# Experts' tokens beyond 128: small blocks of 32 on raw weights in four column groups instead of blocks of 64 on split weights

## The chip, the cores and the metric

One core of a Trainium2 chip runs the whole kernel. The metric is the device time of one execution in microseconds, from its first to its last instruction and what lies around them. Five engines work side by side: TensorE (PE, with its weight loads PEld), VectorE (DVE), ScalarE (ACT), GpSimd (POOL) and SyncE (SP, which here only issues loads). They meet at semaphores. Sixteen DMA engines move data.

## What is computed

One layer of a hybrid decoder for 1024 prompt tokens and 32 sample tokens: a mixer (state space branch and gated MLP branch), cross-attention, then a hierarchical mixture of experts, and a final RMS norm. The change is in the mixture. Cut to what matters:

```python
gid = argmax(xt @ w_rg + b_rg)                      # 1 of 4 groups
top_v, top_i = top_k(le_sel, 2)                     # 2 of its 4 experts
wts = gw * softmax(top_v)
h = silu(xb @ w_eg[e]) * (xb @ w_eu[e])             # 1024 -> 512, per expert e of 16
y[token] += (h @ w_ed[e]) * weight                  # 512 -> 1024
out = rmsnorm(x + y)
```

All in float32. 1056 tokens with two experts each make 2112 token-expert pairs. Worked out from the reference's router on its inputs, the sixteen experts get 181, 136, 180, 169, 115, 128, 120, 117, 128, 155, 130, 113, 135, 91, 125 and 89 of them. Beyond 128 there are tokens at experts 0, 1, 2, 3, 9, 10 and 12: one block of 64 each before, and 2, 1, 2, 2, 1, 1 and 1 blocks of 32 after, 10 in all. The trace of before has the same seven blocks: 96 products of the split kind, 16 a block, make six, and expert 0 has its extra block in the full kind.

## The kernel before, in words

The layer runs in stages. The last two are the router (`router_programs`), which makes tables of which token sits in which slot of which block, and the experts (`stage_experts`, line 3763), where the change is.

**Precision.** A float32 product is made from three fast products: each weight piece (128 x 2048, 1 MB; four pieces for gate and up, two for down, 6 MB an expert) is split into a high part by ACT (`high`, line 4158) and a low part by DVE (`low`, lines 4299 and 4337), and each activation likewise. PE then does high x high, low x high and high x low (`product`, lines 4037 to 4039).

**A full block** has 128 slots. PE's order for block b (`hidden`, `down`, `turn_h`): gate (24 products), up (24), transposes of the next block's gathered rows (line 4024), then down of block b-1 (24), then the transposes of block b's hidden values (line 4105). ACT applies silu, splits, and copies down's result out scaled by the tokens' weights (`out`, line 4203).

**An extra block** of an expert holds up to 64 tokens and comes ahead of the expert's full block. For experts 1 to 14 it is split: the high and the low part of 64 tokens sit side by side in the 128 columns, so two products for each k instead of three (lines 4064 and 4065), and DVE adds the halves (`gated_split`, lines 4312 to 4322). For expert 0 it is a full block.

**POOL** gathers 128 rows of h for a block by an indirect DMA (`gather`, line 3925), and adds the block's result to the residual in DRAM by an indirect DMA that accumulates (`finish`, line 3936), whose landing it waits for before it goes on. Its loop is gather(b+3), finish(b). All blocks go by one number b through all engines, and the inner loops have run-time counts (`start`, `more`, read from the router's tables).

**SP** loads raw weight pieces into six places of 1 MB (`load_piece`), gate and up of expert e as soon as DVE has made the low part of the same place of e-1, down of e-1 after that.

**The tail** loads the residual, makes the norm of all rows, and adds the last two blocks on chip.

Of the kernel before, what the change touches and what calls it, by code (L numbers as in the profile page):

```python
# [23 lines left out]
P = 128  # L24
# [30 lines left out]
XR = 64  # L55
NTHR = (T - P + XR - 1) // XR
NBLK = NE + (2 * (T - P) + 2 * (XR - 1)) // XR + 1
# [2838 lines left out]
def attention_programs(g, qT, kT, vr, oT, mem_o, first, memory, into):  # L2896
# [7 lines left out]
    k_in, v_in = first.k_in, first.v_in  # L2904
    with ExitStack():
# [241 lines left out]
        return Programs(sync, gpsimd, tensor, scalar, vector, s_mm=s_o, s_st=(t_oo, s_mo, sample_turn, sample_values, sample_last, sample_out), sems=None)  # L3147
# [35 lines left out]
def router_programs(g, act_T, w, x, m, memory, att, first, into):  # L3183
# [6 lines left out]
    PW, MB, TQ, LG, PR, CN, TB = 4, 4, 4, 6, 7, 0, 1  # L3190
    NQ = 32
    QG = P // NQ
    NCOL = NBLK + 1
    QC = P // NS
    PAIRS = 2 * NT
    MORE, BASE = 2048, 32768
    BF16 = mybir.dt.bfloat16
    with ExitStack() as ctx:
        g.sb("o_w_offset", [P, 56], ctx=ctx)
# [35 lines left out]
        c9 = g.sb("o_over", [P, NE, NTHR], ctx=ctx)  # L3235
# [5 lines left out]
        step = g.sb("o_steps", [P, NCOL + 1], ctx=ctx)  # L3241
# [4 lines left out]
        past = g.sb("o_past_first", [P, PAIRS], ctx=ctx)  # L3246
        wth = g.sb("o_weights_high", [P, PAIRS], F32R, ctx=ctx)
# [3 lines left out]
        ge = g.alias32("o_reached", [P, PAIRS, NCOL + 1], late)  # L3251
        late += 32 * ((PAIRS * (NCOL + 1) * 4 + 31) // 32)
        ohp = g.alias("o_lane_onehot", [P, PAIRS, P], late)
        ohb = g.alias("o_block_onehot", [P, PAIRS, 3, NCOL], late + PAIRS * P * 4)
        late += PAIRS * P * 4 + 32 * ((PAIRS * 3 * NCOL * 4 + 31) // 32)
        field_i = g.alias_of("o_slot_fields", [P, 4, PAIRS], I32, late)
        field = g.alias32("o_fields", [P, 4, PAIRS], late + 32 * ((4 * PAIRS * 4 + 31) // 32))
# [62 lines left out]
        def gpsimd(pool):  # L3320
# [8 lines left out]
            nc.gpsimd.iota(step[:], [[BASE // 2, NCOL + 1]], 0, 0, **it)  # L3329
# [8 lines left out]
            nc.gpsimd.tensor_scalar(step[:], step[:], 2.0, None, ALU.mult)  # L3338
# [8 lines left out]

            pool.wait_ge(s_inl, 1)
# [7 lines left out]
            pool.wait_ge(s_ge, 1)  # L3356
            nc.gpsimd.tensor_tensor(ohb[:, :, 2, :], ge[:, :, 0:NCOL], last(wtl[:], NCOL), ALU.mult).then_inc(s_ohl, 1)

        def tensor(pe):
# [99 lines left out]
            for i in range(PAIRS):  # L3459
                if i % NT == 0:  # L3460
                    pe.wait_ge(s_oh, i // NT + 1)
                mm = nc.tensor.matmul(ps[:, TB, 0:3 * NCOL], ohp[:, i, :], ohb[:, i].rearrange("p v b -> p (v b)"),
                                      start=(i == 0), stop=(i == PAIRS - 1))
# [294 lines left out]


FAR = 65536.0  # L3760


def stage_experts(g, m):

# [856 lines left out]
```

## Time and profile before

| | us |
|---|---|
| median of 3 runs | 1990.65 (1987.58 to 1990.79) |
| the profiled execution | 1989.6 |
| its span, first to last instruction | 1987.4 |
| first gate product of the experts stage | at 1565.7 |
| last down product | to about 1966 |

The profiled execution is 1.05 us below the median of the runs. Its trace is read by views: the page (one screen for the whole span), windows (busy time of each engine in a stretch), timelines (instructions of one engine in order, with the idle time before each in brackets and what ended it), one source line or one tile (all its instructions, and for DMAs the time from issue to landing).

### The profile page before, as it was taken

The page shows a single profiled execution, that of the slowest core. Times are in us where ns is not written, and L with a number is a line of the kernel's source. Part 1 is how long each engine was busy: PE and PEld are TensorE (multiplying, and loading weights), DVE is VectorE, ACT ScalarE, POOL GpSimd, SP SyncE. Part 2 cuts the span into 40 slices and gives each one's busy share as a digit, 9 for nine tenths or more (in the row PEclk, how much of TensorE's full clock was granted, in tenths as well). Part 3 has the DMA queues.
Part 4 walks back from the last instruction along what each step waited for, and adds up shares of the span by engine and source line. Part 5 has one row for each costly group of instructions (what it writes and reads, how often), then busy time and mean ns, then how long its engine had stood idle before and what let it go on. Part 6 is the DMA issues. An engine that isn't in the chain of part 4 may idle for free. (4 is left out here: it accounts for less than half of the span.)

```text
span 1987.4 us, 32334 instructions
## 1 busy us (share of the span) xinstructions
PE 1912.9 (96%) x11976; PEld 1719.8 (87%) x11977; DVE 1016.1 (51%) x1221; ACT 754.2 (38%) x1105; POOL 405.4 (20%) x513
## 2 busy tenths in 40 slices
PE   7999999999999999999999999999999799999995
PEld 5888999999999999889998799888788788887884
DVE  4314355553556565546114431445544666786785
ACT  4322122222244444523112232433321455775674
POOL 2000100000255545541111000000100221332224
PEclk9999999999999999999999999999999899999998
DMA  6122233333343444498434121446125387998997
GB/s 208 61 92 66 75 86 95 85 86 111 89 129 113 142 119 129 143 316 284 147 105 152 53 75 32 159 170 254 35 94 221 120 270 242 373 382 306 317 315 276
DMA packets 224593, 324.33 MB, mean 163 GB/s; under 512 B 15149, under 2 KB 158029, under 8 KB 224449
## 3 DMA queue, kind: packets, MB, share of 16 engines
q1 hardware_dynamic: 189924, 271.96, 40.1%
q0 software_dynamic: 7344, 25.38, 5.0%
q10 hardware_dynamic: 27232, 25.66, 3.7%
q8 instruction: 69, 1.13, 0.2%
q14 instruction: 24, 0.20, 0.0%
HBM read 250.97 MB, written 73.28 MB: 163 GB/s over the span
## 5 line engine op out<-in xcount | busy, mean ns | idle before, releaser
L4158 ACT ACTIVATE e_w_high<-big 128x2048 fp32r<-128x2048 f32 x94 | 175.5, 1909 | 32.9 <-PEq L3704 20.7
L286 PE MATMUL psum<-hT_high,t_w_high 128*128 128x352 f32 x528 | 171.2, 324 | 0.0
L288 PE MATMUL psum<-hT_high,t_w_low 128*128 128x352 f32 x528 | 170.2, 322 | 0.0
L287 PE MATMUL psum<-hT_low,t_w_high 128*128 128x352 f32 x528 | 170.2, 322 | 0.0
L4299 DVE TENSOR_TENSOR e_w_low<-big,e_w_high 128x2048 fp32r<-128x2048 f32 x64 | 143.8, 2287 | 36.0 <-ACT e_w_high L4158 30.1
L286 PE MATMUL psum<-hT_high,scan_w_high 128*128 128x352 f32 x384 | 131.3, 342 | 0.0
L288 PE MATMUL psum<-hT_high,scan_w_low 128*128 128x352 f32 x384 | 124.5, 324 | 0.0
L287 PE MATMUL psum<-hT_low,scan_w_high 128*128 128x352 f32 x384 | 123.8, 322 | 0.0
L4037 PE MATMUL psum<-e_w_high,e_xT 128*128 128x512 f32 x272 | 107.4, 395 | 3.0 <-DVE e_xT L4295 3.0
L4039 PE MATMUL psum<-e_w_high,e_xT 128*128 128x512 f32 x272 | 106.1, 390 | 0.0
L4038 PE MATMUL psum<-e_w_low,e_xT 128*128 128x512 f32 x272 | 106.0, 390 | 0.0
L286 PE MATMUL psum<-r_w_high,hT_high 128*128 128x512 f32 x256 | 101.6, 397 | 4.5 <-DVE hT_low L720 4.5
L287 PE MATMUL psum<-r_w_low,hT_high 128*128 128x512 f32 x256 | 100.3, 392 | 0.0
L288 PE MATMUL psum<-r_w_high,hT_low 128*128 128x512 f32 x256 | 100.3, 392 | 0.0
L286 PEld LDWEIGHTS psum<-hT_high,t_w_high 128*128 128x128 f32 x528 | 99.1, 188 | 0.1
L287 PEld LDWEIGHTS psum<-hT_low,t_w_high 128*128 128x128 f32 x528 | 99.1, 188 | 0.0
L288 PEld LDWEIGHTS psum<-hT_high,t_w_low 128*128 128x128 f32 x528 | 99.1, 188 | 0.0
L4337 DVE TENSOR_TENSOR e_w_low<-big,e_w_high 128x2048 fp32r<-128x2048 f32 x30 | 67.9, 2290 | 43.5 <-ACT e_w_high L4158 43.5
L1082 DVE SCALAR_TENSOR_TENSOR t_conv_out<-t_conv_in,veca,t_conv_out 128x1080 f32<-128x1080 f32 x60 | 80.7, 1344 | 7.5 <-DVE t_conv_out L1080 1.2
L1525 DVE TENSOR_SCALAR s_att<-psum 128x768 f32<-128x768 f32 x32 | 30.6, 958 | 99.9 <-PE psum L1333 99.9
L286 PE MATMUL psum<-yT_high,m_w_high 128*128 128x352 f32 x252 | 81.6, 324 | 0.0
L287 PE MATMUL psum<-yT_low,m_w_high 128*128 128x352 f32 x252 | 81.4, 323 | 0.0
(623 smaller groups left out, 4971.4 us busy)
## 6 DMA issues: line engine op xcount, KB each, us to landing
big<-in_w_expert_gate SPq DMA_DIRECT2D x32, 1024.0 KB, 7.7
big<-in_w_expert_up SPq DMA_DIRECT2D x32, 1024.0 KB, 9.5
big<-in_w_expert_down SPq DMA_DIRECT2D x32, 1024.0 KB, 12.4
t_w<-in_w_in SPq DMA_DIRECT2D x24, 512.0 KB, 4.7
m_gates<-gate_scr SPq DMA_DIRECT2D x22, 528.0 KB, 4.5
x_scr<-t_conv_out ACTq DMA_DIRECT2D x20, 512.0 KB, 4.6
gate_scr<-s_gate_tanh ACTq DMA_DIRECT2D x16, 528.0 KB, 3.3
scan_w<-in_w_gate SPq DMA_DIRECT2D x16, 512.0 KB, 4.1
```

Of the source, the lines that this page charges most:

```text
L286: nc.tensor.matmul(out, ah, w_h, start=start, stop=False)
L287: nc.tensor.matmul(out, ah, w_l, start=False, stop=False)
L288: return nc.tensor.matmul(out, al, w_h, start=False, stop=stop)
L1082: op = nc.vector.scalar_tensor_tensor(o, c[:, j:j + CB_OUT], wk[j], o, ALU.mult, ALU.add)
L1525: nc.vector.tensor_scalar(att[:, q].rearrange("p (b r) t -> p b (r t)", b=2), ps[:, RB:RB + 2, 0:XW], 0.0, None, ALU.min).then_inc(s_mn, 1)
L4037: nc.tensor.matmul(ps[:, bank, :], ah[:, k, :], w_h, start=(k == 0), stop=False)
L4038: nc.tensor.matmul(ps[:, bank, :], ah[:, k, :], w_l, start=False, stop=False)
L4039: mm = nc.tensor.matmul(ps[:, bank, :], al[:, k, :], w_h, start=False, stop=(k == kt - 1))
L4158: return nc.scalar.activation(dst, src, ACT.Copy)
L4299: nc.vector.tensor_tensor(wl[:, p, :], raw[:, p, :], wh[:, p, :].bitcast(F32), ALU.subtract).then_inc(s_wl, 1)
L4337: nc.vector.tensor_tensor(wl[:, p, :], raw[:, p, :], wh[:, p, :].bitcast(F32), ALU.subtract).then_inc(s_dl, 1)
```

## The change

Every expert now has one full block, and its tokens beyond 128 go into small blocks of 32. A small block is no block of the common numbering; it has tables (`tab_s`, `tw_s`), buffers and semaphores (`z_...`) of its own.

- Its rows are gathered as quarter rows: 32 tokens x 4 quarters of 256 values fill 128 partitions, two transposes on PE turn them. Its result has the same form and is added to DRAM in quarter rows.
- Its products take the raw float32 weights as they were loaded, not the split parts: 128 weight columns move past a stationary 128 x 32 tile of activations, four such products in four column groups of the array. Gate and up take 64 products, down 32. The trace shows a float32 product of this kind as two records.
- gate and up of expert e+1's small blocks come between up and down in PE's turn e, down of the small blocks of e between gate and up of turn e.
- The full blocks' order is fixed: block e is expert e. The experts 1 to 14 run in a loop over pairs, for there are now eight places for raw pieces (two sets for down). Gate and up of e+2 are loaded once the small blocks' gate and up of e+1 are through (`z_gu`); down goes with them.
- The router has 75 table columns instead of 48, 29 thresholds instead of 15, its three products of table entries are all on DVE, and the table product is padded to 256 columns.

```diff
-XR = 64
+XR = 32
 NTHR = (T - P + XR - 1) // XR
-NBLK = NE + (2 * (T - P) + 2 * (XR - 1)) // XR + 1
+NSM = 2 * NTHR
+NCOL = NE + NSM + 1
...
         def _(sp):
+            def load(e, place, n):
+                for p in range(GU):
+                    sp.wait_ge(s_wl, (e - 1) * GU + p + 1)
+                    sp.sem_inc(s_po, 1)
+                    if p == 0:
+                        sp.wait_ge(z_gu, e)
+                        sp.sem_inc(s_po, 1)
                     g.load_piece(sp, e, p)
...
+            def gather_small(s):
+                nc.gpsimd.tensor_copy(idx_z[:], m.tab_s[:, bass.ds(s, 1)]).then_inc(z_ix, 1)
+                pool.wait_ge(z_ix, s + 1)
+                nc.gpsimd.indirect_dma_start(
+                    out=x_s[:], out_offset=None, in_=h_rows,
+                    in_offset=bass.IndirectOffsetOnAxis(ap=idx_z[:, 0:1], axis=0)).then_inc(z_x, 16)
+            def hidden_small(i, s):
+                pool.wait_ge(z_t, s + 1)
+                gather_small(s + 1)
+            def finish_small(i, s):
+                pool.wait_ge(z_o, 2 * s + 4)
...
+                nc.gpsimd.indirect_dma_start(
+                    out=res_rows, out_offset=bass.IndirectOffsetOnAxis(ap=rows_z[:, 0:1], axis=0),
+                    in_=o_s[:], in_offset=None, compute_op=ALU.add).then_inc(z_st, 16)
+                pool.wait_ge(z_st, s * 16 + 16)
+                pool.sem_inc(z_of, 1)
...
-            with pool.Fori(0, before) as b:
-                gather(b + 3)
-                finish(b)
+            def body(e, q, j):
+                first, n = start(pool, e), more(pool, e)
+                if is_(e, 0):
+                    smalls(pool, first, n, hidden_small)
+                smalls(pool, first, n, finish_small)
+                if not is_(e, LAST):
+                    gather(e + 2)
+                    ahead = more(pool, e + 1)
+                    smalls(pool, first + n, ahead, hidden_small)
+                if not is_(e, 0) and not is_(e, LAST):
+                    finish(e - 1)
...
         def _(pe):
+            def hidden_small(e):
+                def do(i, s):
+                    for p in range(GU):
+                        pe.wait_ge(s_w[p], e * 16 + 16)
+                    pe.wait_ge(z_xc, s + 1)
+                    pe.wait_ge(z_hc, s + 1)
...
+                        pe.wait_ge(s_h, e)
...
+                            for q in range(Q4):
+                                mm = nc.tensor.matmul(ps[q * XR:(q + 1) * XR, bank, 0:P], lhs,
+                                                      raw[:, p + k // (DK // 2), at + q * P:at + (q + 1) * P],
+                                                      start=(k == 0), stop=(k == DK - 1))
+                        mm.then_inc(done, 1)
+                    turn_small(s + 1)
+                    pe.wait_ge(z_h, s + 2)
+                    nc.tensor.transpose(ps[:, HT, 0:P], h_s[:], g.ident[:]).then_inc(z_ht, 1)
+                return do
...
+            def body(e, q, j):
+                first, n = start(pe, e), more(pe, e)
...
+                gate(e)
+                if is_(e, 0):
+                    pe.wait_ge(z_tab, 2)
+                    turn_small(0)
+                    smalls(pe, first, n, hidden_small(e))
+                smalls(pe, first, n, down_small(q, j))
+                up(e, first + n)
...
+                    smalls(pe, first + n, ahead, hidden_small(e + 1))
+                if not is_(e, 0):
+                    down(e - 1)
+                pe.wait_ge(z_hc, done + 1)
+                turn_h(e)
...
         def _(act):
+            def out_small(i, s):
+                act.wait_ge(z_of, s + 1)
+                for half in range(2):
+                    act.wait_ge(z_d, 2 * s + 2 + half)
+                    nc.scalar.activation(o_s[:, half * P:(half + 1) * P], ps[:, X + half, 0:P],
+                                         ACT.Copy, scale=m.tw_s[:, bass.ds(s, 1)]).then_inc(z_o, 1)
```

`smalls(eng, first, n, do)` is a loop over n small blocks from number first, with n read at run time. `up(e, done)` ends with a wait for `z_o`, the small outputs of e, and the transposes of block e+1.

The order of POOL, whose copies and DMAs PE waits for. Before, the whole loop body, one turn for each block (L3925 is a gather, L3936 a scatter):

```order
L3922 COPY e_idx<-tab 128x1
L3925 DMA e_x<-h_scr,e_idx 128x1024
L3931 REGISTER_ALU
L3933 ISA
L3933 COPY e_rows<-tab 128x1
L3936 DMA res_scr<-e_out,e_rows 1184x1024
```

Now, from one expert's turn in the loop (L4000 small scatter, L3962 gather, L3983 small gather, L3973 scatter; those with "small" are in loops over small blocks):

```order
L3997 COPY e_small_rows<-tab_small 128x1
L3998 REGISTER_ALU
L4000 DMA res_scr<-e_small_out,e_small_rows 4736x256
...
L3959 COPY e_idx<-tab 128x1
L3962 DMA e_x<-h_scr,e_idx 128x1024
...
L3980 COPY e_small_idx<-tab_small 128x1
L3981 REGISTER_ALU
L3983 DMA e_small_x<-h_scr,e_small_idx 128x256
...
L3970 REGISTER_ALU
L3970 COPY e_rows<-tab 128x1
L3973 DMA res_scr<-e_out,e_rows 1184x1024
```

The small gather stands behind the small scatters and the full gather, and ahead of the full scatter.

The order of ACT between an expert's silu and the weight parts of the next. Before:

```order
L4177 ACTIVATE e_silu<-psum 128x512
L4167 ISA
L4158 ACTIVATE e_w_high<-big 128x2048 x2
L4161 REGISTER_ALU
L4158 ACTIVATE e_xT<-psum 128x8x128
L4158 ACTIVATE e_w_high<-big 128x2048 x2
```

Now:

```order
L4278 ACTIVATE e_silu<-psum 128x512
L3887 COMPARE_AND_BRANCH
L3888 UNCONDITIONAL_BRANCH
L3888 ISA
L4316 ISA
L4318 ISA
L4318 ACTIVATE e_small_out<-psum,tw_small 128x128
L4316 REGISTER_ALU
L4318 ACTIVATE e_small_out<-psum,tw_small 128x128
...
L4263 ACTIVATE e_w_high<-big 128x2048 x2
```

The loop of small outputs (L4318), each of which waits for POOL's scatter of the small block before it, now stands ahead of the next expert's weight parts.

## Rows read from the trace of the kernel before

**Rows 1.** The page: the span, busy shares, and the costliest group (count, busy us, mean ns)
```profile
span 1987.4 us, 32334 instructions
...
PE 1912.9 (96%) x11976; PEld 1719.8 (87%) x11977; DVE 1016.1 (51%) x1221; ACT 754.2 (38%) x1105; POOL 405.4 (20%) x513
...
L4158 ACT ACTIVATE e_w_high<-big 128x2048 fp32r<-128x2048 f32 x94 | 175.5, 1909 | 32.9 <-PEq L3704 20.7
```

**Rows 2.** Windows of the experts stage: engine busy us (instructions), PEclk, DMA share, GB/s
```profile
core 0: us, PE busy (x) PEld busy (x) DVE busy (x) ACT busy (x) POOL busy (x), PEclk, DMA share, GB/s
...
1598.00:1612.30 14.30, 14.30 (x71) 12.05 (x70) 6.98 (x8) 3.29 (x5) 2.08 (x3) 1.00 0.96 318
1710.00:1780.00 70.00, 70.00 (x334) 58.28 (x333) 61.50 (x36) 54.16 (x40) 26.96 (x16) 1.00 1.03 383
1780.00:1795.00 15.00, 12.57 (x61) 10.31 (x60) 10.85 (x7) 8.57 (x6) 5.56 (x4) 1.00 1.03 403
```

**Rows 3.** Timeline of PE: a split block begins, and the next full product begins
```profile
1598.07 0.48 PE L4064 MATMUL psum<-e_w_high,e_xT 128*128 128x512 f32 x1
...
1612.32 0.48 PE L4037 MATMUL psum<-e_w_high,e_xT 128*128 128x512 f32 x1
```

**Rows 4.** Timeline of ACT: the silus of two plain experts in a row
```profile
1699.74 0.60 ACT L4177 ACTIVATE e_silu<-psum 128x512 f32<-128x512 f32 x1 [4.23 <-PE psum L4039]
...
1717.44 0.60 ACT L4177 ACTIVATE e_silu<-psum 128x512 f32<-128x512 f32 x1 [0.61 <-PE psum L4039]
```

**Rows 5.** Line 3365, the router's raw sample product: ns min/median/max, first and last start
```profile
L3365 PE MATMUL psum<-a_w,big x128: 272/273/297, 1458.4 to 1461.8; 128*32 128x128 f32 x128
```

**Rows 6.** Timeline of PE: eight transposes of a gathered block
```profile
1562.34 1.04 PE L4024 MATMUL psum<-ident,e_x 128*128 128x128 f32 x8
```

**Rows 7.** Tile e_x, the gathers of 128 rows
```profile
DMA to landing us min/median/max: 4.3/6.1/9.6
```

**Rows 8.** Line 3936, the scatters that add 128 rows
```profile
DMA to landing us min/median/max: 6.0/10.5/11.5
```

**Rows 9.** Timeline of POOL: one turn of its loop
```profile
1644.17 0.18 POOL L3922 COPY e_idx<-tab 128x1 uint32 x1 [9.94 <-DMA res_scr<-e_out,e_rows]
1645.15 1.01 POOL L3925 DMA_INDIRECT e_x<-h_scr,e_idx  x1 [0.80 <-POOL e_idx L3922]
1646.16 0.20 POOL L3933 COPY e_rows<-tab 128x1 uint32 x1
1647.18 1.58 POOL L3936 DMA_INDIRECT res_scr<-e_out,e_rows  x1 [0.82 <-POOL e_rows L3933]
```

**Rows 10.** Timeline of DVE: the last operation for one plain expert
```profile
1719.10 0.69 DVE L4326 TENSOR_TENSOR e_hT_low<-psum,e_hT_high 128x512 fp32r<-128x512 f32 x1
```

**Rows 11.** Timeline of DVE: two weight parts of the first expert
```profile
1566.27 4.50 DVE L4299 TENSOR_TENSOR e_w_low<-big,e_w_high 128x2048 fp32r<-128x2048 f32 x2 [0.57 <-ACT e_w_high L4158]
```

**Rows 12.** Timeline of POOL: the first and the last of eight index copies
```profile
1580.27 0.18 POOL L3949 COPY e_row_last<-row 128x1 f32 x1 [0.35 <-issue]
...
1585.30 0.18 POOL L3949 COPY e_idx_sample<-e_sample_row 128x1 uint32 x1
```

**Rows 13.** Timeline of PE: three idle times, with what ended them
```profile
1549.71 1.53 PE L3462 MATMUL psum<-o_block_onehot,o_lane_onehot 128*128 128x144 f32 x6 [5.79 <-DVE o_block_onehot L3686]
...
1580.38 0.47 PE L4037 MATMUL psum<-e_w_high,e_xT 128*128 128x512 f32 x1 [1.93 <-DVE e_xT L4295]
...
1793.49 0.50 PE L4037 MATMUL psum<-e_w_high,e_hT_high 128*128 128x512 f32 x1 [2.43 <-DVE e_hT_low L4326]
```

**Rows 14.** Windows behind the first and the third of these
```profile
1549.00:1559.00 10.00, 8.00 (x36) 7.86 (x37) 5.25 (x10) 3.71 (x2) 1.48 (x2) 0.51 0.06 9
...
1795.00:1798.00 3.00, 3.00 (x8) 2.34 (x7) 2.87 (x5) 1.54 (x2) 0.00 (x0) 0.50 1.02 285
```

**Rows 15.** Timeline of DVE: two steps of the router's table arithmetic
```profile
1537.24 0.41 DVE L3646 TENSOR_TENSOR o_over<-o_counts,o_thresholds 128x240 f32<-128x240 f32 x1
...
1543.82 1.07 DVE L3681 TENSOR_TENSOR o_reached<-o_block_at,o_steps 128x864 f32<-128x864 f32 x1
```

More of the change, by code:

```diff
@@ L4106, in turn_h, with turn_small @@
                 tr.then_inc(s_ht, 1)
[L4108 to L4116 removed]
+            def turn_small(s):
+                pe.wait_ge(z_x, s * 16 + 16)
+                for t in range(2):
+                    tr = nc.tensor.transpose(ps[:, SB, t * P:(t + 1) * P], x_s[:, t * P:(t + 1) * P], g.ident[:])
+                tr.then_inc(z_t, 1)
@@ L4287, in _, with body @@
             high(0, 3)
-            each_block(act, plain, last_of, last_high)
+            def body(e, q, j):
+                first, n = start(act, e), more(act, e)
+                if is_(e, LAST):
+                    last_high()
+                silu(e)
+                if is_(e, 0):
+                    smalls(act, first, n, silu_small)
+                    act.wait_ge(z_tab, 2)
+                smalls(act, first, n, out_small)
+                act.sem_inc(z_dn, 1)
+                if is_(e, LAST):
+                    for i in range(2):
+                        square(i)
+                    out_half(LAST, 0, s_d0, s_ob0)
+                    out_half(LAST, 1, s_dn, s_oc)
+                    h_high(LAST)
+                    for i in range(2, NT):
+                        square(i)
+                    last_squares()
+                    return
+                ahead = more(act, e + 1)
+                high(e + 1, 0)
+                high(e + 1, 1)
+                turned(e + 1)
+                high(e + 1, 2)
+                smalls(act, first + n, ahead, silu_small)
+                high(e + 1, 3)
+                if not is_(e, 0):
+                    out(e)
+                down_parts(e, q, j)
+                h_high(e)
+            all_experts(act, body)
         @block.vector
@@ L4425, in summed @@
                                                ALU.mult, ALU.add).then_inc(s_fin, 1)
-            each_block(dve, plain, last_of, at_last)
-            blocks = start(dve, NE - 1) + more(dve, NE - 1) + 1
+            low(0, 0)
+            dve.wait_ge(z_cst, 1 + Q4)
+            nc.vector.tensor_copy(four[:].rearrange("r (q l) -> r q l", q=Q4), mid(g.ident[0:XR, 0:XR], Q4)).then_inc(z_stg, 1)
+            nc.vector.tensor_copy(stg[:, 1, :], ps[0:XR, TABLE_BANK, NCOL + NE:2 * NCOL]).then_inc(z_stg, 1)
@@ L4432, in _ @@
             rows_ready(1)
[L4433 to L4434 removed]
+            summed(0)
+            summed(1)
             for i in range(4, NT):
```

608 lines of the change are left out of this document (300 added, 308 removed).

## The prediction

> **What bounds the kernel now.** I read the page first, then windows, then timelines of the experts stage. The page gives the span and shows PE busy for 96% of it [rows 1]. The windows show that this holds in the stage that changes: inside a split block PE is busy for 14.30 of 14.30 us, in a run of plain experts for 70.00 of 70.00 [rows 2]. So PE is the bound there, but in the plain run the DMA engines are at a share of 1.03 and DVE is busy for 61.50 of 70 us: two others are close behind. In an extra block DVE has 6.98 of 14.30 us to do and ACT 3.29: extra blocks are where the rest catches up.
>
> The prices. A split block takes 1612.32 - 1598.07 = 14.25 us of PE [rows 3]. A plain expert takes 1717.44 - 1699.74 = 17.70 us from silu to silu [rows 4], and a full extra block the same. Raw products in column groups already run in the router: 128 records start from 1458.4 to 1461.8, so 0.027 us each although one lasts 0.273: they overlap [rows 5]. Eight transposes take 1.04 us, 0.13 each [rows 6].
>
> **The work on PE.** Removed: six split blocks, 6 x 14.25 = 85.5, and the extra block of expert 0, 17.7, together 103 us. Added: ten small blocks. Each has 64 + 32 products, at two records each 192, so 192 x 0.027 = 5.2 us, and three transposes and the gaps at the two changes of shape, for which I take 0.6. Ten times 5.8 is 58 us. **Balance -45 us.** If PE never waited, that would be the result. The rest of the sum is waits that the trace of before does not have; all of it is price of hand-overs, because a small block is 5.8 us of work cut by a chain through POOL, DMA, ACT and DVE.
>
> **(a) The small gather.** In PE's turn e the gate and up of the small blocks of e+1 follow the transposes of block e+1, and behind these products PE turns the rows of the next small block, even where this belongs to a much later expert. POOL cannot start that gather early: it has first to gather the next full block, which waits for the same transposes. Copy 0.18, hand-over 0.80, issue 1.01, then copy and hand-over again 1.0 [rows 9]: the small gather is issued 3.0 us after the transposes. Landing: a gather of 128 rows of 4 KB lands in 4.3 to 9.6 us, median 6.1 [rows 7]. One of 128 rows of 1 KB is not in the trace: the same 128 descriptors, a quarter of the bytes, behind a full gather in the same queue. Ends: 3 and 6.1 us; I take 5, nearer the median, because most of it is not bytes. PE has 3.6 us of products meanwhile: 3.0 + 5.0 - 3.6 = 4.4 us of wait. It counts at experts 2, 9, 10 and 12, 4 x 4.4 = 17.5; at 1 and 3 item (c) covers it. For the second small block of 0, 2 and 3 the gather is issued 1.0 us after the turn before: 6.0 against 3.6 of products and 1.3 of copies, 3 x 1.1 = 3. **+20.5** (10 to 30).
>
> The Trainium skill's "DMA: Bandwidth & Descriptors", section "Anatomy of one DMA — SWDGE (gpsimd) path", gives about 2.0 us plus bytes by 436 GB/s, that is 2.3 us for these 131 KB; an estimate by it makes (a) 1.7 us in each of the four places, 7 in all. For the full gather's 524 KB the same formula gives 3.2 us, and this trace has 4.3 as its least.
>
> **(b) DVE is late.** The small down products stand behind gate in turn e and need a copy of the hidden values that stands on DVE behind all of its work for e-1. That ends at 1719.10 + 0.69 = 1719.8 [rows 10], while the gate product is done before ACT's silu at 1717.44 [rows 4]. So 2.4 us plus the copies, 2.7, at six experts (all with small blocks but 0). **+16** (10 to 20).
>
> **(c) Two small blocks in one expert (0, 2, 3).** The output buffer is single: ACT may write the second output once POOL has seen the first scatter land. Copy and hand-over 1.0, landing of a scatter that adds: 6.0 to 11.5, median 10.5, for 4 KB rows [rows 8]; for 1 KB rows I take 6, between 4.5 (the least, less a quarter) and the median. PE has the second down, 1.7, and up, 5.5, meanwhile. And POOL itself comes late, from the full block's scatter, which it waits out before. I take 4 us for each, 12. Worse is what stands behind on ACT: the next expert's high parts, 2 x 1.9 [rows 1], then DVE's low part 2.3 and the gating 0.7, which the next small products wait for (`s_h`). That is 6.8 us after the second output; PE has 0.8 of transposes: 6 us, three times, 18. **+30** (6 to 42).
>
> **(d) The start.** The first small gather waits for the small tables and the sample rows on DVE, now behind the first expert's weight parts, which end at 1566.27 + 4.50 = 1570.8 [rows 11], then for POOL's eight copies, 1580.27 to 1585.5 with two of them slowed, 1.5 if none is [rows 12]. 1571.5 + 3.4 + 1.0 + 5.0: it lands at about 1581, and PE stands in front of it from 1571.2, with up of expert 0 queued behind. Less the 1.9 us that PE lost there before [rows 13]: 8, and the second block's hand-overs 1. **+9** (5 to 13).
>
> **(e) The clock.** After 5.79 us of idle PE the granted clock was 0.51 of full for 10 us, that is the lower of the two levels, 1.2 GHz; after 2.43 us it was 0.50 for 3 us; after 1.93 us it stayed at 1.00 [rows 13, 14]. Waits of 4 us and more will be about nine. At 1.5 us lost for each it is 14, and about half of the slow stretches meet another wait: **+8** (0 to 46).
>
> **(f) The router.** 240 elements of thresholds in 0.41 us become 464, 864 elements of steps in 1.07 become 1350 [rows 15]; a third multiply comes to DVE from POOL, a slow one beside it is gone. **+2** (1 to 4). The table product has 256 columns instead of 144 and is hidden in the same wait.
>
> **Nothing for the rest.** The loads: 6 MB an expert as before. Gate of e+2 is now issued some 6 us later (behind the third low part), down one expert earlier; with waits in most turns the queue has the room. Between experts 4 and 8 it has none (share 1.03), see rival 3. The tail is unchanged.
>
> **Sum.** -45 + 20.5 + 16 + 30 + 9 + 8 + 2 = +40.5 us on the profiled execution's 1989.6: 2030. The median lies 1 us above that execution: **2031 us**, slower by 2%. Of the ten small blocks each saves 4.5 us of work and brings about 8.5 us of waits.
>
> **Rivals.**
>
> 1. *The hand-overs are cheap: faster.* The one mechanism: small indirect DMAs land fast, 3 us for the gather, 4.5 for the scatter. Then (a) is 10, the wait for the scatter is over before up is, so (c) falls to 3 x 2, (d) is 5, the clock stays up, (b) is 12: -45 + 10 + 12 + 6 + 5 + 0 + 1 = -11, 1980 us. It decides from the point where waits are under 4.5 us for each small block. For it: a quarter of the bytes. Against it: the full gather, whose 0.52 MB are worth 1.3 us at 403 GB/s [rows 2], needs 4.3 at least [rows 7], and POOL's serial order is there in any case. By the skill's formula above the gathers would be in this case; nothing in the sum hangs on it. Chance 0.13.
> 2. *The clock stays down: much slower.* If each of nine waits brings a stretch like the one at 1549, 5.1 us lost apiece, (e) is 46: 2068 us. For it: nearly every turn from 0 to 3 and 9 to 12 has two or three waits. Against it: after 2.43 us it was 3 us only. Chance 0.17.
> 3. *The loads become the bound.* Later gate loads in the plain run, at share 1.03: experts 4 to 9 take some 1.7 us more each, and the small products of 9 and 12 wait for raw up pieces, 8 to 10 us in all: 2040 us. Chance 0.10.
> 4. *The column groups do not overlap as said.* Four times 5.2 us a block: +156, 2187 us. The same shape overlaps in the router [rows 5]. Chance 0.02.
>
> The forecast itself: 0.56. The other 0.02 is something else.
>
> **Range.** 1996 to 2062. Its low end gives two thirds of the way from the forecast to rival 1, the high end nearly all of the way to rival 2; what lies outside is most of rival 1 and half of rival 2, about 2 in 10. A measurement of this kernel can tell some 0.2% (4 us) from no change. Faster by more than that: most of rival 1, 0.10; the same 0.03; slower 0.87.
>
> **What would show it.** In the profile after: 1920 product records with 32-column weights (10 x 192) at about 0.027 us start to start; PE busy down by some 45 us and idle up by some 80 in the experts stage; among its waits those for the small gather (transposes of e_small_x) of 4 us, about four of them, one of 8 to 10 at the start, and three pairs for the small output and for e_h at experts 0, 2, 3. PEclk below 1 in several stretches of the stage. Landing of the small gather 5 us, of the small scatter 6. Wrong would be: PE idle in the stage under 50 us; small landings under 3.5 us; POOL done long before PE asks; or a stage bound by loads with ACT waiting for raw pieces in most turns.

## The result

The changed kernel takes **2052.3 us** (median of 4 runs, 2050.9 to 2053.5) against 1989.1 for the one before: a ratio of 1.032, 95% interval 1.030 to 1.0335. It is slower, by 63 us where 41 were forecast. The profiled execution has a span of 2049.8 us, 62.4 more than before. The page of the changed kernel:

```profile
span 2049.8 us, 35905 instructions
...
PE 1899.7 (93%) x13430; PEld 1708.1 (83%) x13431; DVE 1001.0 (49%) x1243; ACT 741.8 (36%) x1106; POOL 417.0 (20%) x534
...
PE   7999999999999999999999999999996778987894
...
PEclk9999999999999999999999999999998889998997
```

Against [rows 1] PE's busy time fell by 13 us only, though 45 us of work were to go, and its share from 96 to 93%. From the 31st slice on, where the experts are, PE is at 6 to 9 tenths and the granted clock at 8 or 9, where it was at 9 before that. The stage from the first gate product to expert 15's silu, as windows of the kernel before and of the changed one:

```profile
core 0: us, PE busy (x) PEld busy (x) DVE busy (x) ACT busy (x) POOL busy (x), PEclk, DMA share, GB/s
1565.70:1947.20 381.50, 376.47 (x1774) 312.80 (x1775) 277.10 (x183) 240.59 (x183) 104.17 (x95) 1.00 0.88 304
```

```profile
1564.70:2000.60 435.90, 361.82 (x3227) 301.18 (x3228) 256.95 (x203) 228.11 (x184) 116.52 (x109) 0.91 0.73 258
```

PE stood still for 5 us of the stage before and for 74 now (the window less PE's busy time), and its clock was at 0.91 in the mean. No other engine came near being the bound: DVE's and ACT's busy time fell, and so did the DMA share.

**How the time is split below.** For each kernel the stage is cut into three terms that add up to it. *Idle*: the gaps over 0.25 us between PE's matmul records. *Clock*: half of the time that PE was busy while the granted clock was at its lower level of 1.2 GHz (0.50). Half is a round share: in the changed kernel a product of 512 columns takes 0.427 us from start to start at the lower level and 0.227 at 2.4 GHz, so 0.47 would be nearer, and its term 25 instead of 27. *Work*: what is left. The tail is what lies behind the stage. The split comes from one profiled execution of each kernel. Eight of the kernels below have the small blocks and the same products as the changed one, and their work comes out at 334 to 339 us: a few us of difference in the work or clock term say nothing.

```
kernel            median us   stage = work + idle + clock   tail
before              1989.1    381.5 = 374.8 +  5.0 +  1.7   40.2
changed             2052.3    436.0 = 336.0 + 73.1 + 26.9   49.1
```

So the stage's +54.5 us are **work -38.8, idle +68.1, clock +25.2**. The stage begins 1.0 us earlier than before, and the tail is 8.9 us longer. That is the whole of the 62.4 by which the span grew.

**The waits.** What PE waited for in the stage, by the view of waits (line and tile, released by, us in total, times, longest):

```profile
PE psum L4214 <- DVE e_small_hT L4460: 24.1, 8, 4.8
PE psum L4193 <- DVE e_h L4413: 17.3, 5, 6.4
PE psum L4172 <- DMA e_small_x<-h_scr,e_small_idx: 15.4, 7, 4.7
PE psum L4193 <- DMA big<-in_w_expert_up: 7.3, 1, 7.3
PE psum L4105 <- ACT e_small_out L4318: 2.6, 1, 2.6
```

Line 4214 is the small down product, 4193 the small gate and up, 4172 the transposes of the small rows, 4105 those of the full rows. Ten small blocks bring 14 waits of 1.8 to 7.3 us, twelve of them of 3.4 and more, and some shorter ones. The first row is the largest, and the timeline shows what it is, at expert 2:

```profile
1653.06 0.23 DVE L4453 COPY e_small_hT_first<-psum 128x64 f32 x1
...
1661.78 4.50 DVE L4423 TENSOR_TENSOR e_w_low<-big,e_w_high 128x2048 fp32r<-128x2048 f32 x2 [5.96 <-ACT e_w_high L4263]
...
1666.31 0.69 DVE L4417 TENSOR_TENSOR e_hT_low<-psum,e_hT_high 128x512 fp32r<-128x512 f32 x1
1668.17 0.20 DVE L4459 COPY e_small_hT<-e_small_hT_first 128x64 f32 x1 [1.17 <-issue]
...
1668.62 0.66 PE L4214 MATMUL psum<-big,e_small_hT 128*32 128x128 f32 x8 [4.11 <-DVE e_small_hT L4460]
```

The hidden rows are in SBUF at 1653.3. Their copy into the tile that the down products read takes 0.2 us, but it is queued on DVE behind the low halves of the down weights, the low part of the full rows and 1.2 us in which DVE waits for nothing that the profile shows (the program has two register loads there). It comes 15 us later, and PE waits 4.1. DVE was not short of time: it stood idle for 5.96 of these 15 us, until ACT had made the high halves of the down weights, with the copy behind them on its queue.

**The clock.** Two groups of the same 128 products, in full and at the lower clock:

```profile
1861.56 3.70 PE L4193 MATMUL psum<-big,e_small_xT 128*32 128x128 f32 x128 [0.86 <-DVE e_h L4413]
```

```profile
1826.34 6.09 PE L4193 MATMUL psum<-big,e_small_xT 128*32 128x128 f32 x128 [7.31 <-DMA big<-in_w_expert_up]
```

```profile
1861.50:1865.26 3.76, 3.70 (x128) 3.46 (x128) 1.00 0.37 101
1826.30:1832.45 6.15, 6.09 (x128) 5.85 (x128) 0.60 0.90 360
```

At 1.00 a record takes 3.70 / 128 = 0.029 us from start to start, with four column groups side by side, near the router's 0.027 [rows 5]. After 7.31 us of idle PE the clock was 0.60 in the mean of the next window, and the same work took 6.09. The stage has 13 stretches at the lower level, 75.1 us together, and PE was busy for 53.9 of them. Most of that, 45.7 us, was products and transposes of the small blocks: they stand right behind the waits, so they meet the low clock first.

**The landings** of the small gather (line 3983) and of the small scatter (line 4000), issue to landing, min/median/max:

```profile
DMA to landing us min/median/max: 2.8/2.8/4.6
```

```profile
DMA to landing us min/median/max: 3.8/3.8/8.1
```

The medians were put too long in the prediction, at 5 and 6. Single ones differ: the two small scatters of expert 0 and that of expert 1 took 8.1, 5.3 and 6.4. By the formula of the Trainium skill's "DMA: Bandwidth & Descriptors", section "Anatomy of one DMA — SWDGE (gpsimd) path", that the prediction set beside (a), the small gather takes 2.3 (an estimate); the trace, with 2.8, is half a microsecond above it.

**The tail.** POOL at the end of the changed kernel, and the ACT operation that waits behind it:

```profile
1990.64 2.19 POOL L3959 COPY e_idx<-tab 128x1 uint32 x1 [9.43 <-issue]
1993.67 2.22 POOL L3962 DMA_INDIRECT e_x<-h_scr,e_idx  x1 [0.84 <-POOL e_idx L3959]
1995.89 1.39 POOL L3970 COPY e_rows<-tab 128x1 uint32 x1
1998.06 2.83 POOL L3973 DMA_INDIRECT res_scr<-e_out,e_rows  x1 [0.78 <-POOL e_rows L3970]
...
2010.89 1.06 ACT L4333 ACTIVATE e_x<-big 32x1024 f32<-32x1024 f32 x1 [9.61 <-DMA big<-res_scr]
```

The gather at 1993.67 is a 17th one, whose rows no product reads. The last full scatter, which the final norm waits for, stands behind it; it was issued 2.5 us before the stage's end, against 6.9 before (1940.33 of 1947.2).

### The profile page after: what moved, and what is told of

Read it like the earlier page. It is cut to its first block and busy times, and to the rows that moved or that the text cites. A ratio compares the mean times of both kernels' runs of the same rounds, so it can differ in the third digit from the quotient of the medians.

```text
span 2049.8 us, 35905 instructions
## 1 busy us (share of the span) xinstructions
PE 1899.7 (93%) x13430; PEld 1708.1 (83%) x13431; DVE 1001.0 (49%) x1243; ACT 741.8 (36%) x1106; POOL 417.0 (20%) x534
## 5 line engine op out<-in xcount | busy, mean ns | idle before, releaser
L4118 PE MATMUL psum<-e_w_high,e_xT 128*128 128x512 f32 x256 | 103.2, 403 | 3.3 <-issue 1.8
L4119 PE MATMUL psum<-e_w_low,e_xT 128*128 128x512 f32 x256 | 100.9, 394 | 0.0
L4120 PE MATMUL psum<-e_w_high,e_xT 128*128 128x512 f32 x256 | 100.7, 393 | 0.0
L289 PE MATMUL psum<-yT_high,m_w_low 128*128 128x352 f32 x252 | 81.0, 321 | 0.0
```

Of the source, the lines that this page charges most:

```text
L289: return nc.tensor.matmul(out, al, w_h, start=False, stop=stop)
L4118: nc.tensor.matmul(ps[:, bank, :], ah[:, k, :], w_h, start=(k == 0), stop=False)
L4119: nc.tensor.matmul(ps[:, bank, :], ah[:, k, :], w_l, start=False, stop=False)
L4120: mm = nc.tensor.matmul(ps[:, bank, :], al[:, k, :], w_h, start=False, stop=(k == kt - 1))
```

## The experiments

All change the changed kernel, but for e6, which changes the one before. The time is the median of the runs, the terms are those of the profiled one.

```
kernel                                  median us   stage = work + idle + clock   tail
changed                                   2052.3    436.0 = 336.0 + 73.1 + 26.9   49.1
e1  products in waits, 54 a turn          2089.9    474.7 = 411.2 + 46.2 + 17.4   50.2
e8  the same, 22 a turn                   2044.4    428.9 = 366.6 + 47.4 + 15.0   50.2
e5  no small blocks                       1916.8    301.2 = 279.5 + 17.6 +  4.1   43.8
e6  before, no extra blocks               1899.6    293.7 = 277.4 + 13.8 +  2.5   38.7
e2  small gather first                    2043.7    429.6 = 339.2 + 66.5 + 23.9   48.7
e9  e2, no 17th gather                    2038.7    431.4 = 338.1 + 67.9 + 25.4   44.9
e3  small down later                      2074.2    460.9 = 334.2 + 98.9 + 27.8   45.1
e7  e3 and e9                             2036.8    429.7 = 335.5 + 67.5 + 26.6   45.0
e10 hidden rows copied earlier            2042.9    425.2 = 336.3 + 69.5 + 19.5   51.6
e11 e9, e10, later wait for e_h           2025.1    419.6 = 337.0 + 57.8 + 24.8   43.6
e12 e11, scatters not waited for          2004.7    396.6 = 338.5 + 43.0 + 15.0   43.0
e13 e12, first small rows earlier         2003.0    392.6 = 337.4 + 40.3 + 15.0   42.7
```

### Is the slow clock a cost of its own? (e1, e8)

```
+                if not is_(e, 0):
+                    with pe.If(n > 0):
+                        g.keep_busy(UP, 34)
                 smalls(pe, first, n, down_small(q, j))
...
+                    with pe.If(ahead > 0):
+                        pe.wait_ge(s_sg, e + 1)
+                        g.keep_busy(GA, 20)
                     smalls(pe, first + n, ahead, hidden_small(e + 1))
```

> The changed kernel, and TensorE works while it waits: 34 products of the identity with itself (128x128) ahead of an expert's small down products, 20 ahead of the next expert's small gate and up products, both only for an expert that has small blocks; nothing reads them. Clock theory: the stage from the first gate product to expert 15's silu ran 75 us at half the granted clock against 3 us before, and that cost some 31 of its 54 us; what drops it are the waits of 3 to 7 us at the small blocks. Then the stretches at 0.5 shrink to under 40 us and the kernel is 10 to 18 us faster than the changed one (2034 to 2042 us), although some of the added products last longer than the wait that they fill. Waits theory: the time is that of the waits alone and a slow clock only runs through idle time; then the kernel is no faster than the changed one, 2050 to 2056 us.

Measured: 2089.9 us, 37.6 slower than the changed kernel, which neither theory had. A product is two records of 0.11 us, so the 324 of them took at least 0.22 us each, not the 0.13 of a transpose [rows 6] that I had sized them by: 75 us more work, which replaced 27 us of idle time. The terms still speak: clock fell by 9.5 us. It was repeated with 14 and 8 in place of 34 and 20, 132 products:

> The changed kernel with fewer products in the waits: 14 ahead of the small down products and 8 ahead of the next small gate products of an expert with small blocks (34 and 20 cost 75 us at 0.22 us each, for 27 us of gaps and 19 us of slow busy time gone). 132 products are 30 us, in about 41 us of waits. Clock theory: of the slow busy time (54 us) some 15 to 20 go, 8 to 10 us are won and at most 5 lost where a wait is shorter than its filling: 2041 to 2050 us. Waits theory: no gain from the clock, 2052 to 2060.

Measured: 2044.4 us, **7.9 faster than the changed kernel, with 30.6 us more work on PE**. The products replaced 25.7 us of idle time, so by the waits alone it would be 5 us slower; the clock term fell by 11.9. The stage's window:

```profile
1564.10:1993.00 428.90, 380.82 (x3491) 322.70 (x3492) 256.80 (x203) 227.71 (x184) 117.38 (x109) 0.96 0.74 262
```

The mean granted clock is 0.96 instead of 0.91. The clock theory holds: the lower clock slowed work and didn't only run through idle time. The time is in that theory's range and below the other's 2052. Against the kernel before the intervals of the ratio are apart, 1.0262 to 1.0297 for e8 and 1.030 to 1.0335 for the changed kernel.

### What do the small blocks cost as a whole? (e5, e6)

```
-            nc.vector.tensor_copy(m.more[:], nbk[:])
+            ts(m.more[:], nbk[:], 0.0, None, ALU.mult)
```

and in the same way `m.start` (set to zero in e5, to the expert's number in e6, with `m.behind` one less). Both kernels leave out the part of the output that these blocks give.

> The changed kernel with the counts of small blocks set to zero: the ten small blocks are not computed (their part of the output is left out), the 16 full blocks, the loops and the tables stay. It measures what the ten small blocks cost as a whole. The work of the ten is 58 us of TensorE at full clock; by the trace they also bring 68 us of gaps and some 31 us of slow clock, together about 157 us. So 1890 to 1905 us if all gaps and the slow clock come from the small blocks; above 1915 if a part of them belongs to the 16 full blocks under the new static order.

> The kernel before with its extra blocks left out: the count of blocks beyond an expert's first is set to zero and block e is expert e's, so the part of the output that the extra full blocks give is left out; loops, splits and last block stay. Against the changed kernel without its small blocks (1916.8 us) it shows what the static order and the new hand-overs cost with no extra block anywhere. Theory: the static order itself is nearly free, so 1905 to 1925 us, and the whole loss stands in the small blocks: about 135 us for ten against some 75 for the extra blocks before. Rival: the static order of 16 blocks costs or saves over 15 us, then below 1900 or above 1930.

Measured: 1916.8 and 1899.6 us. Ten small blocks cost 2052.3 - 1916.8 = 135.5 us, in the stage 56.5 of work, 55.5 of idle and 22.8 of clock. The extra blocks of before cost 1989.1 - 1899.6 = 89.5 us, all of it work (97.4 in the stage, with 8.8 us of idle *removed*). So 46 of the 63 us are the small blocks. The other 17 are there with no extra block in either kernel. Of these the profiles show 7.5 us in the stage, 5.1 in the tail and 0.5 at the start, 13 in all; the other 4 are spread from run to run, since e5's profiled execution lies 2.0 us below its median and e6's 2.7 above. The rival of e5 was right (1916.8 against 1915), and 1899.6 stands at the edge of e6's (1896.8 to 1902.3 against 1900): the static order, with what came along with it, is not free.

The two subtractions have a limit. Without extra blocks the loads bind a part of the stage: ACT waits for raw weight pieces, for 45 us in e6's stage and 69 in e5's, against 13 in the kernel before and 13 in the changed one. In e5:

```profile
ACT e_w_high L4263 <- DMA big<-in_w_expert_gate: 36.5, 24, 11.3
ACT e_w_high L4263 <- DMA big<-in_w_expert_up: 32.2, 15, 2.7
```

Its last plain experts are 19.0 us apart from silu to silu, nine times in a row, instead of 17.7 [rows 4], and from 1700 to 1855 us the DMA share is 1.03 in both kernels. That is the mechanism of rival 3, in kernels without extra blocks. So an extra block also gives the loads time to catch up, and 135.5 and 89.5 us are what the blocks add to a stage that is partly bound by loads, not their whole bill on PE.

### Where does the gather stand on POOL's queue? (e2, e9)

```
-                smalls(pool, first, n, finish_small)
                 if not is_(e, LAST):
-                    gather(e + 2)
                     ahead = more(pool, e + 1)
-                    smalls(pool, first + n, ahead, hidden_small)
+                    with pool.If(ahead > 0):
+                        hidden_small(0, small_of(first + n))
+                smalls(pool, first, n, finish_small)
+                if not is_(e, LAST):
+                    gather(e + 2)
...
```

and behind it the gathers of the expert's other small blocks.

> The changed kernel, with one step moved on GpSimd's queue: the gather of the next expert's first small block is issued ahead of this expert's small scatters and of the full gather, instead of behind them. If the small transposes and small gate products wait for that gather's landing because it is queued behind a scatter's landing (3.8 us) and a full gather, the waits ahead of the small transposes (15.2 us in six) and some of those ahead of the small gate products go: 8 to 15 us less, 2037 to 2044 us. Rival: the gather waits for the small rows of the expert before to be turned anyway, and lands as late: at most 3 us less, 2049 to 2053.

Measured: 2043.7 us, 8.6 less, the low end of what the theory had. The waits ahead of the small transposes fell from 15.4 us in seven to one, that at the start: the queue order was their cause.

```profile
PE psum L4177 <- DMA e_small_x<-h_scr,e_small_idx: 4.7, 1, 4.7
```

> Small gather first (2043.7 us) and the 17th full gather left out, which no product reads but which stands ahead of the last full scatter on GpSimd's queue. If the last scatter is late because of it (issued at 1998.06 in the changed kernel, 50 us before the end, and ScalarE waits 9.6 us for the rows behind it), the tail shortens by 4 to 7 us: 2037 to 2040. Rival: the scatter before it holds the queue as long, and the tail stays at 48 to 49 us, within 2 us of 2043.7.

Measured: 2038.7 us, in the range. The tail went from 48.7 to 44.9, so by 3.8, a little less than the 4 to 7 expected; the last scatter's issue now is at 1988.12 of a stage that ends at 1993.5, 5.4 us ahead of its end instead of 2.5. The theory holds.

### Why does PE wait ahead of the small down products? (e3, e7, e10)

The first idea was that the products stand too early on PE's queue:

```
-                smalls(pe, first, n, down_small(q, j))
                 up(e, first + n)
+                pe.wait_ge(s_oc, e)
+                smalls(pe, first, n, down_small(q, j))
```

(with the banks DN for X, ACT's `out_small` behind `turned(e + 1)`, and DVE's first `down_small` ahead of `gated(e)`)

> The changed kernel, with the small down products moved behind the up products and the next expert's transposes (they stood between gate and up), into the banks of the full down product; VectorE adds a first small block's quarters ahead of the gated product, ScalarE copies the small output behind the transposed rows. Theory: the 25.1 us of waits ahead of the small down products go, since the hidden rows then have 6 us more, and with them the slow clock behind them: gaps 20 to 30 us fewer, the time 25 to 40 us less than the changed kernel's (2012 to 2027). Rival: the outputs, the scatter and the next block's buffers come as much later, and the waits reappear ahead of the small gate products and the full down product: within 5 us of the changed kernel.

Measured: 2074.2 us, 22 *slower*. The two largest waits in its stage:

```profile
PE psum L4171 <- DMA e_small_x<-h_scr,e_small_idx: 51.8, 7, 10.9
PE psum L4213 <- DVE e_small_hT L4463: 20.7, 7, 6.0
```

The theory fell: 20.7 us ahead of the down products stayed, and 51.8 ahead of the small transposes came, since POOL issues the next small gather behind the small scatter, and that had become later. The rival had the waits come back elsewhere, which they did, but ahead of the small transposes, which it didn't name, and it put the cost far too low.

> Both moves at once, with the unneeded 17th gather left out: the next expert's first small gather ahead on GpSimd's queue, the small down products behind up and the transposes. With the small down products later alone, 51.8 us of waits stood ahead of the small transposes, since the gather was queued behind a scatter that now came later. Theory: gather first takes that away (some 45 us) and with it 10 us of slow clock, so gaps of 45 to 60 us and 2000 to 2025 us. Rival: the transposes wait for something else (the rows' buffer, ScalarE's queue), and the time stays above 2040.

Measured: 2036.8 us, neither the theory's 2000 to 2025 nor the rival's 2040 and more. The small gather's waits fell to 13.8 us as the theory said, but against e9, which has all of it but the later down products, the gain is 1.9 us, less than the spread of e9's runs (2037.0 to 2043.4), and 21.3 us of waits ahead of the down products are still there. So moving them on PE's queue wins nothing that can be seen. The copy of the hidden rows had moved on DVE only from one late place to another. Hence the copy itself, moved alone:

```
                 smalls(dve, first + n, ahead, hidden_small)
                 dve.sem_inc(z_gu, 1)
+                with dve.If(ahead > 0):
+                    down_small(0, small_of(first + n))
                 low(e + 1, 3)
```

> The changed kernel with one step moved on VectorE's queue alone: the copy of the first small block's hidden rows that its small down products read is issued right behind their transposes, one expert earlier, instead of behind that expert's low halves of the down weights and of the hidden rows and two register loads. In the trace of the changed kernel those rows are there at 1653.4 us and are copied at 1668.2, while TensorE waits 4.1 us from 1664.5. Theory: TensorE's 25.1 us of waits ahead of the small down products fall to under 8, and with them 5 to 12 us of slow clock, so 2022 to 2036 us. Rival: ScalarE's and VectorE's queues behind stay as late, and the wait turns up ahead of the next small gate products (VectorE's gated product waits for the low halves): then 2040 to 2050.

Measured: 2042.9 us. Its waits:

```profile
PE psum L4172 <- DMA e_small_x<-h_scr,e_small_idx: 22.8, 6, 5.9
PE psum L4193 <- DVE e_h L4413: 20.2, 5, 6.4
...
PE psum L4214 <- DVE e_small_hT L4460: 6.6, 3, 2.9
```

24.1 us became 6.6, so DVE's queue was the cause. But the waits for the small gather rose by 7.4 us and those for `e_h` by 2.9: the idle term fell by 3.6 in all. **Most of the wait went to where POOL was late.** The time is the rival's, but not the place, which it put ahead of the small gate products. The 9.4 us won are for the most part the clock term, which fell by 7.4: there are 8 slow stretches instead of 13. The tail is 2.5 us longer, for a reason that isn't known.

### Are the terms separate? (e11, e12, e13)

e11 adds to e9 and e10 one move: PE waits for the gated product (`s_h`) between the small gate and the small up products, not ahead of both.

> The changed kernel with four moves: the hidden rows copied earlier on VectorE, the first small gather first on GpSimd's queue, no 17th gather, and TensorE waiting for the gated product only between the small gate and the small up products instead of ahead of both. If the waits are separate terms: 2038.7 (gather moves alone) less about 22 for the down waits with their clock, less 10 for the wait moved behind the small gate products (1.9 us in each of some five waits of 3.8 to 6.4 us): 2000 to 2015 us. Rival: one wait gives way to the next and the moves together bring no more than the best of them, 2025 us or above.

Measured: 2025.1 us (2014.2 to 2029.7), at the rival's edge. But the moves do bring more together than the best of them alone. Against the changed kernel e9 wins 13.6 us and e10 9.4, together 23.0; e11, with the third move, wins 27.2. What the moves brought alone nearly adds up; the forecast was too low because it took 22 us for the hidden rows' copy, which alone brought 9.4. Idle is down to 57.8, and a new wait is the largest:

```profile
PE psum L4114 <- DMA e_x<-h_scr,e_idx: 12.7, 3, 6.1
PE psum L4181 <- DMA e_small_x<-h_scr,e_small_idx: 12.1, 4, 4.6
PE psum L4114 <- ACT e_small_out L4327: 7.1, 2, 4.5
```

Now the full gather is late, and again POOL issues it: POOL stands still until each scatter has landed, in this run's median 5.7 us for a small one and 9.8 for a full one. In e12 it doesn't:

```
                     in_=ob[:], in_offset=None, compute_op=ALU.add).then_inc(s_o, 16)
-                pool.wait_ge(s_o, b * 16 + 16)
-                pool.sem_inc(s_of, 1)
...
+            def full_landed(e):
+                pool.wait_ge(s_o, (e - 1) * 16)
+                pool.sem_inc(s_of, 1)
```

`full_landed` stands ahead of the next small scatter, and the wait for the last small scatter behind the full gather.

> The four moves of before (2025.1 us), and GpSimd no longer stands still until a scatter has landed: it issues the gathers first and waits for the landing (small 3.8 us, full 10.3 us in the median) only ahead of the next scatter. In the trace with the four moves TensorE waits 19.8 us in all ahead of the full transposes (12.7 of them for the gather's landing) and 12.1 us for the small gather. Theory: GpSimd's queue is what the waits of the new static order come back to, so these 25 us fall to under 10, and with them 6 to 10 us of slow clock: 1998 to 2010 us. Rival: the landings compete (a gather issued beside a scatter in flight lands later), or the outputs' buffers come free later: 2018 us or above.

Measured: **2004.7 us**, 20.4 less than e11 by this move alone (18.3 when each is set against the kernel before as run beside it, 1990.0 and 1987.9); idle -14.8, clock -9.8. The theory holds: no wait for the full gather is left, and 4.7 us for the small one, at the start. The largest that remain:

```profile
PE psum L4218 <- DMA big<-in_w_expert_up: 11.4, 2, 7.6
PE psum L4218 <- DVE e_h L4438: 6.6, 2, 3.8
PE psum L4239 <- DVE e_small_hT L4485: 6.6, 3, 2.9
```

The largest is for the raw weights of up, which the small products need before the full block of the same expert would: the loads of rival 3. Issuing them earlier was not tried. The rival of e12 is true in part, and costs less than is won: the landings of the small gather and of the small scatter, issue to landing, became

```profile
DMA to landing us min/median/max: 2.8/5.9/7.2
```

```profile
DMA to landing us min/median/max: 3.8/5.0/8.7
```

Of the 11 small gathers the four that were issued with a full scatter in flight landed in 6.9 to 7.2 us, and each landed behind that scatter. Five took 2.8. The other two took 5.9 and 6.1 with no scatter in flight at their issue, as the same two did in e11. Whether the four queue behind the scatter or share something with it stays open.

> The kernel with the scatters not waited for (2004.7 us), and one step moved at the start: GpSimd issues the gather of the very first small block as soon as its table is there (1567.06 us in that trace), ahead of the eight small copies, which wait for a table that VectorE finishes at 1572.3; it was issued at 1574.29 behind them, and TensorE waited 4.65 us for it from 1572.5. Theory: that wait goes, with 2 to 4 us of slow clock behind it: 1997 to 2001 us. Rival: the next thing at the start is as late (the first raw weights, VectorE's copy of the transposed rows behind the tables), and 3 of the 4.65 us come back: 2002 to 2006 us.

Measured: 2003.0 us (median of 6 runs; ratio to before 1.0043 to 1.0076; that of e12 is 1.006 to 1.0094). The profile shows the wait of 4.65 us gone, one of 2.1 for small rows in its place and the stage 4.0 us shorter; the medians differ by 1.7 us, which can't be told from nothing. The term is small and stays open between 0 and 4 us.

No version beat the kernel before. The best one is slower by 0.6% (0.4 to 0.8), with 37 us less of work on PE in the stage.

## Why the prediction was right, and where it was off

The sign was right, the range (1996 to 2062) held the time, and the mechanism was the one forecast: a small block is cut into hand-overs, and PE waits at them. The profiled execution came out 21.9 us above the sum: clock +17.2, tail +8.9, work +6.2, idle -7.4, router -3.0. By the steps:

- **Work, -45:** it was -38.8. By e5 and e6 a small block is 5.65 us of work (5.8 forecast) and what was removed is 97.4 us, not 103; these two numbers come from stages that loads bind in part.
- **(a) The small gather, +20.5:** 10.5 us. The landing was put at 5 us and is 2.8. Of the four waits of 4.4 us two came, 4.75 at expert 2 and 3.4 at expert 10. The queue order behind them was right (e2 took them all).
- **(d) The start, +9:** 4.7 us.
- **(b) DVE late, +16:** 25.1. The place and the cause were right (e10). The 2.4 us from the gate product to the end of `e_hT_low` are there (1664.55 to 1667.0 at expert 2), but the 1.2 us behind it, where DVE's register loads stand, were not counted. So five waits are 4.1 to 4.8 us instead of six of 2.7; the sixth, at expert 1, didn't come. The other 3.4 us are four smaller ones, at experts 0, 2 and 3.
- **(c) Two small blocks in one expert, +30:** about 15. For the scatter 12 us were forecast, and 2.6 came, at expert 0, whose first small scatter landed in 8.1 us. At experts 2 and 3 it landed in 3.8. For what stands behind on ACT and DVE 18 were forecast, three times 6. Two such waits came, 6.4 and 4.4 us, and one of 1.8 behind expert 1. The third could not come: behind expert 3's small blocks expert 4 has none that would wait.
- **Not in the sum:** 12 us ahead of the small gate products of experts 9, 10 and 12, of which 7.3 for a raw up piece. Rival 3 had that wait, "8 to 10 us in all", with a chance of 0.10; the other half of it, 1.7 us more for each plain expert, came only in part: 18.1, 17.7, 18.3 and 19.1 us from silu to silu of experts 4 to 8, against 17.7 [rows 4].
- **Idle altogether, +75.5:** +68.1. That these agree is luck: (a) and (d) were twice too large, (c) too, (b) too small by a third, and 12 us were missing.
- **(e) The clock, +8: this is the step that was furthest off, and the largest part of the error.** It is +25.2. The prediction counted nine waits of 4 us and more, took 1.5 us lost for each, 14 us, and halved that, since "about half of the slow stretches meet another wait". In fact the stage has 13 slow stretches. Each of the twelve waits of 3.4 us and more has one, and one more stands behind three waits of 0.7 to 1.3 us. 2.1 us are lost in each, and there was no ground for halving: PE was busy for 54 of the 75 us. Rival 2 is that mechanism at 46; the truth lies in the middle of the two. e8 shows the term apart from the waits.
- **(f) The router, +2:** the stage begins 1.0 us earlier. This says little: with the router of the changed kernel it began at 1562.1 to 1566.8 in other profiled executions.
- **"The tail is unchanged": wrong, +8.9.** 5.1 are there without any small block (e5 against e6). The 17th gather is worth 3.8 (e9), and since e5 has it too, the two numbers don't add up to a full account: the rest stays open. The change's static loop issues a gather two experts ahead also where there is none; that could be read in the code.
- **Rival 1** asked for landings of 3 and 4.5 us and gave 1980 us. The landings were 2.8 and 3.8 in the median, and the time was 2052. Among the prediction's signs of being wrong stood "small landings under 3.5 us", and for the gather it came true. For (a) and (d) rival 1 was right: it had 10 and 5, and 10.5 and 4.7 came. It failed at what a short landing does not shorten: (b) at 12 and (c) at 6, where PE waits for DVE or ACT to come to the step, and the clock at 0.

## What to carry to other kernels

Price a small piece of work by the chain around it: ten blocks of 5.7 us cost 13.6 each. A hand-over's wait is set less by how long the transfer or copy takes than by what stands ahead of it on its queue, above all by a queue that stands still for a landing. When one wait is taken away, part of it comes back on the next late queue, so look at the whole list of waits again and not only at the one that was moved: in e10 17.5 us went and the idle term fell by 3.6. The largest gain, 20 us, was in not standing still for landings; it was measured only on top of the other moves, so what it brings alone isn't known.

## What was not expected of the hardware

- Waits cost about a third more than their length: 73 us of idle PE brought 27 us of clock, and in the other kernels with small blocks the clock term is 0.28 to 0.43 of the idle term. Work that nobody reads, laid into waits that were there anyway, made the kernel faster (e8): 30.6 us of it for -7.9 us.
- A float32 product of the 128x128 identity with itself is two records of 0.11 us, so 0.22 us or more (e1, e8); a transpose by it is one record, 0.13 in a group of eight [rows 6].
- A small indirect gather issued while a full scatter is in flight lands in 6.9 to 7.2 us instead of 2.8 (four of eleven in e12).
